# Two-layer hybrid decoder: the convolution taps of odd hidden tiles moved behind the twelve additions of part one, and an even order of those additions

## What is computed

```
def conv_glu_ffn(h, w_up, conv_w, w_down):
    gu = h @ w_up
    g, u = jnp.split(gu, 2, axis=-1)
    g = causal_dwconv(g, conv_w)
    return (jax.nn.silu(g) * u) @ w_down

def reference(x, ...):
    for layer in range(DEPTH):
        h = h + hybrid_mixer(rms_norm(h, norm_mix_g[layer]), ...)
        h = h + conv_glu_ffn(rms_norm(h, norm_ffn_g[layer]), ...)
    return rms_norm(h, final_g)
```

## Time and profile before

| | us |
|---|---|
| median of three runs | 2472.76 |
| lowest and highest | 2470.64, 2473.79 |
| the profiled execution | 2474.76 |
| its span in the trace | 2472.8 |
| PE busy | 2370.1 |
| DVE, POOL, ACT busy | 1692.8, 1338.5, 994.4 |

### The profile page before, as it was taken

The page is one execution under the profiler, slowest core; times in us unless marked ns, Lnnn a source line. Parts: engine busy times, 40 slices in busy tenths (PEclk is TensorE's granted clock), DMA queues, the critical chain, the costliest instruction groups (busy, mean ns, idle before and its releaser), DMA issues.

```text
span 2472.8 us, 32208 instructions
## 1 busy us (share of the span) xinstructions
PE 2370.1 (96%) x11340; PEld 1960.9 (79%) x11340; DVE 1692.8 (68%) x2641; ACT 994.4 (40%) x1896; POOL 1338.5 (54%) x893
## 2 busy tenths in 40 slices
PE   7999999999999999999999999999989999999998
PEld 6888888777777777777778888878767777777776
DVE  8654777738677776667795557785586777777765
ACT  4344444525333334334423344443353433333333
POOL 3222323447677777777542222342677777777774
PEclk9999999999999999999999999999999999999999
DMA  9956786321233333333398668742123333333332
GB/s 286 223 140 158 202 194 137 105 63 41 89 95 94 94 94 93 95 90 94 124 284 201 162 154 209 182 100 75 60 60 94 90 94 90 96 99 96 94 94 77
DMA packets 162766, 304.45 MB, mean 123 GB/s; under 512 B 11440, under 2 KB 31024, under 8 KB 162608
## 3 DMA queue, kind: packets, MB, share of 16 engines
q1 hardware_dynamic: 129408, 238.20, 30.8%
q0 software_dynamic: 31616, 62.92, 14.2%
q10 hardware_dynamic: 1584, 1.28, 0.2%
HBM read 292.66 MB, written 135.27 MB: 173 GB/s over the span
## 4 chain that ended last, share of the span: by engine, by line
PE 58%; DVE 20%; POOL 14%; ACT 4%; issue 4%; DMA 1%; DVEq 0%; POOLq 0%; ACTq 0%; SPq 0%
PE ps L1015 7%; PE ps L1017 7%; PE ps L1016 7%; PE ps L1044 6%; PE ps L1046 6%; PE ps L1045 6%; POOL w_lo L758 5%; DVE k_next L2399 3%; PE ps L1358 3%; PE ps L1122 3%; PE ps L1124 3%; PE ps L1123 3%; POOL mix_raw L829 3%; PE ps L1345 2%; DVE h L1954 2%
## 5 line engine op out<-in xcount | busy, mean ns | idle before, releaser
L758 POOL TENSOR_TENSOR w_lo<-more_stage,w_hi 128x512 fp32r<-128x512 f32 x304 | 452.1, 1487 | 216.0 <-ACT w_hi L1799 204.5
L723 POOL CAST w_hi<-stage 128x1024 fp32r<-128x1024 f32 x68 | 73.2, 1077 | 683.2 <-PE ps L1017 612.1
L1015 PE MATMUL ps<-x_hi,w_hi 128*128 128x512 f32 x928 | 375.7, 405 | 7.6 <-DVE q_next L1927 4.8
L1017 PE MATMUL ps<-x_hi,w_lo 128*128 128x512 f32 x928 | 365.5, 394 | 0.0
L1016 PE MATMUL ps<-x_lo,w_hi 128*128 128x512 f32 x928 | 364.5, 393 | 0.0
L1799 ACT ACTIVATE w_hi<-more_stage 128x512 fp32r<-128x512 f32 x294 | 184.0, 628 | 391.7 <-PE ps L1046 260.5
L1044 PE MATMUL ps<-T_hi,w_hi 128*128 128x512 f32 x688 | 269.8, 392 | 7.9 <-DVE q_next L2372 6.5
L758 POOL TENSOR_TENSOR w_lo<-stage,w_hi 128x512 fp32r<-128x512 f32 x146 | 212.2, 1453 | 116.1 <-ACT w_hi L1799 108.8
L1045 PE MATMUL ps<-T_lo,w_hi 128*128 128x512 f32 x688 | 269.0, 391 | 0.0
L1046 PE MATMUL ps<-T_hi,w_lo 128*128 128x512 f32 x688 | 268.9, 391 | 0.0
L1954 DVE TENSOR_TENSOR h<-ps,h 128x512 f32<-128x512 f32 x400 | 249.0, 679 | 0.3
(11 more groups left out here) (274 smaller groups left out, 4972.2 us busy)
## 6 DMA issues: line engine op xcount, KB each, us to landing
summed<-stream SPq DMA_DIRECT2D x40, 1024.0 KB, 10.2
more_stage<-stream SPq DMA_DIRECT2D x128, 256.0 KB, 2.7
stage<-stream SPq DMA_DIRECT2D x52, 512.0 KB, 3.6
more_stage<-summed SPq DMA_DIRECT2D x100, 256.0 KB, 2.6
summed_downs<-stream SPq DMA_DIRECT2D x16, 1280.0 KB, 10.7
summed<-stream POOLq DMA_DIRECT2D x20, 1024.0 KB, 15.5
summed<-summed POOLq DMA_DIRECT2D x20, 1024.0 KB, 13.0
more_stage<-summed_downs SPq DMA_DIRECT2D x60, 256.0 KB, 2.6
```

Of the source, the lines that this page charges most:

```text
L758: pool.tensor_tensor(block_of(w_lo, n), raw, block_of(w_hi, n).bitcast(f32), ALU.subtract)\
L1015: pe.matmul(out, w_hi[:, s, w], hi, start=start, stop=False)
L1017: return pe.matmul(out, w_lo[:, s, w], hi, start=False, stop=stop)
```

## The change

Five edits, all in the feed-forward part:

1. DVE's part one additions come in another order: the first CHAINED bank, then the four SINGLE banks (two each), then the other three CHAINED banks. The waits of PE follow.
2. The taps of every odd tile but the last move from `combine` (and `second_tile`) behind those twelve additions; `add_product` 7 now comes ahead of the taps, in even tiles too.
3. ACT rounds the two blocks of part one ahead of `silu`, not behind it.
4. In the first pair two `add_product` steps of tile 1 move ahead of T4's rests, and ACT keeps tile 1's first product ahead of tile 0's `silu`.
5. A layer's last tile goes through `silu`, `value` and its rounding in halves of 512 positions (`last_halves`, new on ACT and DVE), with semaphores of its own.

```
@@ products and part_b on PE
-                        pe.wait_ge(add_done, added + ROWS + 2 * (SINGLE.index(b) + 1))
+                        pe.wait_ge(add_done, added + 1 + 2 * (SINGLE.index(b) + 1))
...
-                    pe.wait_ge(add_done, added + m + 1)
+                    pe.wait_ge(add_done, added + (1 + 2 * ROWS + m if m else 1))
@@ last_down on PE
-                        pe.wait_ge(mix_ready, 2 * layer + 2)
+                        pe.wait_ge(last_lo, 2 * layer + 1)
...
+                pe.wait_ge(last_lo, 2 * (layer + 1))
@@ prepare_ffn on ACT
-                silu()
+                act.wait_ge(conv_ready, seen(conv_ready))
                 act.sem_inc(first_kept, 1)
                 keep_first_product(layer, 1)
+                act.activation(k_next[:, :], k_next[:, :], ACT.Silu).then_inc(silu_done, 1)
@@ ACT
+            def last_halves(layer):
+                act.wait_ge(conv_ready, seen(conv_ready))
+                for t in halves_of_t:
+                    act.activation(k_next[:, t], k_next[:, t], ACT.Silu).then_inc(last_silu, 1)
+                act.wait_ge(down_done, layer * DOWNS + (PAIRS - 1) * PAIR_DOWNS)
+                for n, t in enumerate(halves_of_t):
+                    act.wait_ge(last_value, 2 * layer + n + 1)
+                    act.activation(mix_hi[1][:, t], k_next[:, t], ACT.Copy).then_inc(last_hi, 1)
...
                     elif what == "part_a":
+                        round_blocks(2)
                         silu()
-                        round_blocks(2)
@@ DVE
             def add_part_a():
-                add_rows(CHAINED, (0, 0, False))
-                add_rows(SINGLE, (ROWS, 1, False), (0, 1, True))
+                dve.wait_ge(down_done, downs[0] + 1)
+                add_row(0, CHAINED[0], 0, 0, False)
+                for m, b in enumerate(SINGLE):
+                    dve.wait_ge(down_done, downs[0] + ROWS + m + 1)
+                    add_row(m, b, ROWS, 1, False)
+                    add_row(m, b, 0, 1, True)
+                for m, b in enumerate(CHAINED[1:], 1):
+                    add_row(m, b, 0, 0, False)
+                downs[0] += PART_A_DOWNS
...
                 form("T4", 3, "T2", "B21", ALU.subtract)
+                low_gates, high_ups = padded[:, PAD:PAD + HALF], q_next[:, HALF:]
+                add_product(layer, 1, 5, low_gates, 0, low_gates)
+                add_product(layer, 1, 5, low_gates, 2, high_ups)
                 for k in rows:
                     rest("T4", k)
...
                 add_product(layer, f, 6, low_ups, 3, low_ups, first_kept)
-                convolve_gates(layer, f)
-                dve.sem_inc(conv_ready, 1)
-                add_product(layer, f, 7, high_ups, 2, high_ups)
+                if f < F_TILES - 1:
+                    add_product(layer, f, 7, high_ups, 2, high_ups)
+                    if f % 2 == 0:
+                        convolve_gates(layer, f)
+                        dve.sem_inc(conv_ready, 1)
+                else:
+                    convolve_gates(layer, f)
+                    dve.sem_inc(conv_ready, 1)
+                    add_product(layer, f, 7, high_ups, 2, high_ups)
...
+            def last_halves(layer):
+                for n, t in enumerate(halves_of_t):
+                    dve.wait_ge(last_silu, 2 * layer + n + 1)
+                    dve.wait_ge(combined, sums[0])
+                    dve.tensor_tensor(k_next[:, t], k_next[:, t], q_next[:, t], ALU.mult).then_inc(last_value, 1)
+                for n, t in enumerate(halves_of_t):
+                    dve.wait_ge(last_hi, 2 * layer + n + 1)
+                    dve.tensor_tensor(mix_lo[1][:, t], k_next[:, t], mix_hi[1][:, t].bitcast(f32), ALU.subtract)\
+                       .then_inc(last_lo, 1)
...
                     elif what == "part_a":
                         add_part_a()
+                        convolve_gates(layer, 2 * n + 1)
+                        dve.sem_inc(conv_ready, 1)
                         value()
```

More of the change, by code:

```diff
@@ L837, in form_t1 @@
                 done = layer * (PAIRS - 1) + pair
-                pool.wait_ge(value_ready, layer * F_TILES + 2 * pair + 1)
+                pool.wait_ge(value_ready, layer * (F_TILES - 1) + 2 * pair + 1)
                 if pair:
@@ L850, in form_t2_t3 @@
                 done = layer * (PAIRS - 1) + pair
-                pool.wait_ge(value_ready, layer * F_TILES + 2 * pair + 2)
+                pool.wait_ge(value_ready, layer * (F_TILES - 1) + 2 * pair + 2)
                 pool.wait_ge(t_rested, 4 * done + 1)
@@ L1176, in part @@
                                       mix_hi[f][:, halves_of_t[t]], mix_lo[f][:, halves_of_t[t]], f == 0, f == 1)
-                pe.wait_ge(mix_ready, 2 * layer + 1)
+                pe.wait_ge(mix_ready, layer + 1)
                 pe.wait_ge(add_done, half_added(layer, 0, 0) - 1)
@@ L1563, in keep_first_product @@
                 if f > 1:
-                    act.wait_ge(value_ready, layer * F_TILES + f)
+                    act.wait_ge(value_ready, layer * (F_TILES - 1) + f)
                 act.wait_ge(product_done, PRODUCTS * (layer * F_TILES + f) + 1)
@@ L1803, in center @@
                 if f == F_TILES - 1:
-                    act.wait_ge(mix_ready, 2 * layer + 1)
+                    act.wait_ge(mix_ready, layer + 1)
                 elif f % 2:
@@ L1913, in _ @@
                     else:
-                        silu()
-                        keep_value(F_TILES - 1, mix_hi[1], layer * DOWNS + (PAIRS - 1) * PAIR_DOWNS)
+                        last_halves(layer)
                 if layer < DEPTH - 1:
@@ L1943, in absorb, with add_row, add_rows @@
                                              ALU.mult, ALU.subtract).then_inc(x_lo_ready, 1)
-            def add_rows(banks, *outs):
+            def add_row(m, b, rows, t, taken):
+                row = h[:, rows + m, halves_of_t[t]]
+                if taken:
+                    dve.tensor_tensor(row, row, bank(b), ALU.subtract).then_inc(add_done, 1)
+                else:
+                    dve.tensor_tensor(row, bank(b), row, ALU.add).then_inc(add_done, 1)
+            def add_rows(banks, out):
                 for m, b in enumerate(banks):
                     dve.wait_ge(down_done, downs[0] + 1)
[L1949 to L1954, removed]
+                    add_row(m, b, *out)
                     downs[0] += 1
             def add_part_a():
-                add_rows(CHAINED, (0, 0, False))
-                add_rows(SINGLE, (ROWS, 1, False), (0, 1, True))
+                dve.wait_ge(down_done, downs[0] + 1)
[7 more added lines that the diff above has]
+                downs[0] += PART_A_DOWNS
             def add_part_b():
@@ L2354, in second_tile @@
                 add_product(layer, 1, 7, u3, 2, low_gates, taken=True)
-                convolve_gates(layer, 1)
-                dve.sem_inc(conv_ready, 1)
+                dve.wait_ge(combined, sums[0])
+                dve.sem_inc(gate_ready, 1)
             def add_product(layer, f, n, other, b, out, kept=None, taken=False):
@@ L2435, in feed @@
                     else:
-                        value()
-                        value_rest(F_TILES - 1)
+                        last_halves(layer)
             def next_norm(layer):
```

9 lines of the change are left out of this document (3 added, 6 removed).

## The result

The changed kernel takes 2528.01 us (median of four runs, 2525.06 to 2529.77), the kernel before 2471.7 (2470.6 to 2473.79). The ratio is 1.0226, with a 95% interval of 1.0208 to 1.0243: it is slower, by 56 us, where 66 were forecast (2539, range 2493 to 2562). The profiled execution has a span of 2526.5 against 2472.8.

The account below looks back on a forecast made before the run. PE was taken as the bound, busy 2370.1 of 2472.8 us, so a change wins only its waits. Later pairs +75.6, first pairs −6.9, layer ends −2.6 gave +66: 2539 us, range 2493 to 2562.

Parts of the forecast that it names:

- The term that decides: POOL's in-order queue up to A12's block starts late behind the odd tile's value: period 63.26 against 59.06, +75.6 over eighteen pairs.
- S: The moment when PE could start the even tile, behind the last matmul of part one; 921.30 in the pair read.
- The first pairs: First pair of each layer: A12 starts 4.9 earlier in layer one, 2.0 in layer two; together −6.9 us.
- The sum: All terms over the whole kernel: 75.6 − 6.9 − 2.6 = +66 us, added to the median 2472.76.
- The start of the even tile: PE at S: it waits for three additions in the new order, S stands, and 0.95 is won per pair.
- the layer ends: Each layer's last tile: halves remove waits of 1.1 on the last rest, with slow restart 1.3 each; −2.6 us.
- The even taps' collisions: POOL's chain beside DVE's even taps: these move with it and meet the same rests; both delays taken (2.28 and 2.27).
- My first rival: POOL's operations slip between DVE's, so collisions fall apart: +0.85 to +2.3 a pair, 2478 to 2505; chance 0.15.
- The rule of the Trainium skill: DVE and POOL exclusion on SBUF: four collisions cost 0.27 more each, 1.1 a pair, total 20 higher; not in the sum.
- The clock: Rival: PE's clock falls in most pairs, in its two new stands; 2562 and up; chance 0.08.
- The waits by size: PE's new waits: some 0.8 ahead of T3, 2 to 3 ahead of S2, 1 to 2 ahead of A12; POOL's some 7.

Follow-up runs that it names:

- order-only run: Kernel before with only the even order of part one's additions and the two PE waits that go with it; 2446.39 us, ratio 0.9902.
- taps put back: Changed kernel with the taps back ahead of the additions in all hidden tiles but tile 1; 2441.66 us, ratio 0.988.
- one-tap run: Changed kernel without the second of the two taps of every even hidden tile from 2 on; 2515.93 us, ratio 1.0179.

## Why the prediction was right

**The term that decides** held in its mechanism and within 0.4 us a pair. Its steps, measured from S, as forecast and as seen: start of the taps 4.85 and 4.74; end of `silu` 8.65 and 8.50; end of the value's product 9.95 and 9.76; POOL's block 5 from 9.35 and 9.09, T2 and T3 from 13.9 and 13.57, A12's start 27.75 and 27.33. The period was put at 63.26 and is 62.83. Of this 0.43, 0.26 was there by POOL's start on block 5, and 0.17 came in block 6, which took 2.23 beside the value's rest, not 2.4. The measured time is 11 us under the one forecast; the size was off, the path was not.

**The first pairs** came right in sum, −6.5 against −6.9, by two errors that offset each other. The two executions must first be put on one clock: tile 0's taps, which stand ahead of any edit, start at 594.26 before and at 591.30 in the changed kernel, and the matmuls there are 2.97 earlier too. With 2.97 added, S of layer one is 617.95, 1.45 later than the 616.5 forecast. T1's rest on POOL, on which that sum was built, came 1.67 later than in the kernel before, not 0.4 (610.77 + 2.97 = 613.74 against 612.07). The step that was missed is on ACT. Before:

```profile
595.28 1.28 ACT L1815 ACT_TABLE_LOAD   x1
598.55 1.06 ACT L1815 ACTIVATE k_next<-k_next 128x1024 f32<-128x1024 f32 x1 [1.99 <-DVEq L2330]
```

And in the changed kernel:

```profile
595.67 0.60 ACT L1569 ACTIVATE padded<-ps 128x512 f32<-128x512 f32 x1 [3.37 <-DVEq L2352]
596.29 1.28 ACT L1638 ACT_TABLE_LOAD   x1
597.58 1.06 ACT L1638 ACTIVATE k_next<-k_next 128x1024 f32<-128x1024 f32 x1
```

I had charged the copy of 0.60 that now stands ahead of `silu`. But ACT also loads its function table for `silu`, 1.28 us. Before, it did so while it waited for the taps; now the load stands behind the copy and ahead of `silu`, with no wait to hide it, and `silu` ends at 598.64, on the common clock 601.61, 2.0 later than before. So A12 came 3.9 earlier in layer one, not 4.9. In layer two S came 1.5 later than forecast as well, but there the error lay in the kernel before too: from S to A12 its first pair took 24.22, not the 22.60 of the later pairs, so A12 came 2.6 earlier, not 2.0. The reason is the clock. PE before, in that pair:

```profile
1841.43 0.46 PE L1044 MATMUL ps<-B_hi,w_hi 128*128 128x512 f32 x1
1841.68 0.63 PE L1045 MATMUL ps<-B_lo,w_hi 128*128 128x512 f32 x1
```

The first matmul behind the stand of 3.90 took 0.50, which I read as a clock that had not fallen. It fell three matmuls later: from 1842 to 1844 the granted clock was 0.50, and some eight matmuls started 0.43 apart.

**The sum.** The span grew by 53.7 where the terms gave 66. Of the 12.3 between them 7.7 are the period (18 × 0.43). Another 0.6 is the second pair of each layer, whose wait on the subtraction had been 1.11 and not 0.79, so that more went with it. 3.0 is the time by which the execution shown was early ahead of any edit, and 1.8 lies behind the last pair, in the final normalization, where the kernel before had more matmuls at the lower clock; neither is known to be of the change. The first pairs took 0.4 back, and what is left is under 0.5.

**The start of the even tile** and **the layer ends** held. The first is shown alone by the order-only run. For the ends, the last period is 57.96 with halves (taps put back) and 59.23 without (order only), 1.27 a layer for the 1.3 forecast.

**The even taps' collisions** were taken at 0.98 and 0.97, and 2.27 twice is what POOL shows, 889.00 and 891.23; leaving one tap out gave 0.98 back. My first rival, collisions falling apart, was wrong here for the reason given: T2's rest and the taps both hang on T4. It is no rule of the kernel: with the blocks of part one behind `silu` the taps started behind these two rests, which took 1.28 and 1.29. The rule of the Trainium skill ("SBUF — State Buffer", "Who interferes with whom") that a VectorE instruction with two SBUF inputs contends with a GpSimd instruction that reads SBUF agrees with the trace: the value's product held up block 5, and the even taps held up two rests. The page has the second one blocked until the first ends, and a DMA issued from GpSimd some 115 ns longer. POOL's rests waited less than that: block 5 started at 875.36 beside a product that ended at 876.03, and took 1.82 where 1.30 is usual, 0.52 for 0.67.

**The clock** was priced as a rival of its own, from 2562, and its chance was lowered by a wrong reading: it had followed the stand of 3.90 too (above). In the changed kernel it did fall in ten pairs of twenty, and cost almost nothing, since another wait stood behind it. The forecast had both facts and did not put them together: a stretch at the lower clock that ends ahead of a longer wait is paid for already. Where that wait was cut, in the one-tap run, the price appeared.

**The waits by size**: 0.8 ahead of T3 was 0.41, 2 to 3 ahead of S2 was 2.35, 1 to 2 ahead of A12 was 1.45 (in ten pairs; in the ten others the slow matmuls stood in its place), POOL's for block 5 6.83 for 7. The one ahead of the seventh product (0.38) was not listed.

## What to carry to other kernels

An engine's list is a queue: before you make something on it later, look at what stands behind it and does not need it. Here two weight blocks behind a late `silu` cost 69 us, and putting them ahead of it took most of the loss away, while the wait that the change removed was worth 20 (18 × 1.09). And an order that is right with one neighbour can be wrong with the next: the even order of additions gained 25 us with the taps ahead and cost 35 with them behind.

## What the runs showed of the chip

- The same stand of PE, 2.33 us at the same place in the pair, is followed by the lower clock in some pairs and not in others (granted 0.66 and 1.00), and a stand of 5.4 to 5.5 was followed by it in all twenty pairs. The fall need not show in the first matmul: behind the stand of 3.90 it came three matmuls later.
- A DVE operation with two SBUF operands and a POOL one delay each other both ways: the tap 1.28 to 2.20, POOL's rest 1.30 to 2.27. Where POOL idled, two odd taps took 2.60; with work moved there they took 3.51.
- ACT's load of a function table, 1.28 us, costs nothing where it falls into a wait, as before at 595.28. With a copy put ahead of `silu` it stood on the path, at 596.29.
